# The last two rows of an output projection, taken bank by bank, and a running total of squares over seven banks

## What is computed

```python
def rms_norm(x, g):
    xf = x.astype(jnp.float32)
    y = xf * lax.rsqrt(jnp.mean(xf * xf, axis=-1, keepdims=True) + EPS)
    return (y * g.astype(jnp.float32)).astype(x.dtype)

for l in range(DEPTH):                                  # DEPTH = 2
    ...
    mixed = jnp.concatenate([y, m_out], axis=-1) @ w_out[l]
    h = h + rms_norm(mixed, norm_mix_post[l])
    f = swiglu_ffn(rms_norm(h, norm_ffn_pre[l]), w_ffn_in[l], w_ffn_out[l])
    h = h + rms_norm(f, norm_ffn_post[l])
...
# second block
y, yc = token_mix(h, hc, lp, with_ctx)                  # ends in ... @ w_out
x = x + gate1 * rmsnorm(y, g_post_mix[l])
```

## Time and profile before

| | us |
|---|---|
| median of 3 runs | 1951.76 |
| lowest and highest run | 1950.09, 1953.26 |
| span of the profiled execution | 1947.3 |
| PE busy (matmuls) | 1814.3 (93% of the span) |
| DVE busy | 1216.2 (62%) |
| ACT busy | 896.1 (46%) |
| POOL busy | 125.7 (6%) |

### The profile page before, as it was taken

The page is one execution under the profiler, slowest core; times in us unless marked ns, Lnnn a source line. Parts: engine busy times, 40 slices in busy tenths (PEclk is TensorE's granted clock), DMA queues, the critical chain, the costliest instruction groups (busy, mean ns, idle before and its releaser), DMA issues.

```text
span 1947.3 us, 25641 instructions
## 1 busy us (share of the span) xinstructions
PE 1814.3 (93%) x9201; PEld 1507.9 (77%) x9201; DVE 1216.2 (62%) x2170; ACT 896.1 (46%) x1452; POOL 125.7 (6%) x137
## 2 busy tenths in 40 slices
PE   7997999999999997899999999799987989999997
PEld 7875788888887865678888888678576878888885
DVE  3554668887323656456865532564575479889888
ACT  3446443222213445543223221342383368888885
POOL 1000000000000000000110000120000210110102
PEclk8898999999999998999999999799998879999999
DMA  4223225455333124024655423330011359999995
GB/s 150 87 76 115 87 64 142 134 145 147 107 96 96 44 65 184 23 65 137 182 159 149 119 93 97 112 89 22 21 67 66 108 222 377 395 385 370 386 372 187
DMA packets 203854, 289.32 MB, mean 149 GB/s; under 512 B 12332, under 2 KB 150548, under 8 KB 203636
## 3 DMA queue, kind: packets, MB, share of 16 engines
q1 hardware_dynamic: 188788, 239.56, 36.9%
q0 software_dynamic: 11920, 36.48, 6.1%
q10 hardware_dynamic: 3056, 12.06, 1.6%
HBM read 271.77 MB, written 21.53 MB: 151 GB/s over the span
## 4 chain that ended last, share of the span: by engine, by line
PE 85%; DVE 7%; ACT 6%; issue 1%; DMA 1%; POOL 0%; DVEq 0%; ACTq 0%; POOLq 0%
PE bank L200 23%; PE bank L202 23%; PE bank L201 23%; PE bank L69 11%; PE bank L654 2%; DVE weights_low L227 1%; PE bank L2195 1%; ACT weights_high L221 1%; DVE tmp L69 1%; DVE z_and_u L69 1%; DVE ring L69 1%; PE bank L1651 1%; ACT spare L69 1%; PE bank L2544 1%; PE bank L272 1%
## 5 line engine op out<-in xcount | busy, mean ns | idle before, releaser
L227 DVE TENSOR_TENSOR weights_low<-ring,weights_high 128x1024 fp32r<-128x1024 f32 x202 | 246.7, 1223 | 395.3 <-ACT weights_high L221 394.8
L200 PE MATMUL bank<-XH,weights_high 128*128 128x512 f32 x1056 | 423.2, 401 | 17.8 <-DVE weights_low L227 6.5
L202 PE MATMUL bank<-XH,weights_low 128*128 128x512 f32 x1056 | 415.6, 394 | 0.0
L201 PE MATMUL bank<-XL,weights_high 128*128 128x512 f32 x1056 | 415.2, 393 | 0.0
L221 ACT CAST weights_high<-ring 128x1024 fp32r<-128x1024 f32 x202 | 211.1, 1047 | 432.6 <-PE bank L202 422.8
L200 PEld LDWEIGHTS bank<-XH,weights_high 128*128 128x128 f32 x1056 | 200.8, 190 | 63.0 <-DVE weights_low L227 9.6
L202 PEld LDWEIGHTS bank<-XH,weights_low 128*128 128x128 f32 x1056 | 200.7, 190 | 43.4
L201 PEld LDWEIGHTS bank<-XL,weights_high 128*128 128x128 f32 x1056 | 201.1, 190 | 40.3 <-issue 0.5
L2235 DVE TENSOR_TENSOR XL<-ring,XH 128x1024 fp32r<-128x1024 f32 x144 | 169.8, 1219 | 11.7 <-ACT XH L2229 11.7
L2229 ACT CAST XH<-ring 128x1024 fp32r<-128x1024 f32 x144 | 145.2, 1048 | 0.6 <-PE bank L202 0.6
L69 DVE SCALAR_TENSOR_TENSOR squares<-ring,c_silu,squares 128x128 f32<-128x128 f32 x384 | 135.2, 352 | 13.6
(11 more groups left out here) (506 smaller groups left out, 3263.2 us busy)
## 6 DMA issues: line engine op xcount, KB each, us to landing
ring<-in_w_ffn_in SPq DMA_DIRECT2D x88, 512.0 KB, 4.7
ring<-in_w_gate SPq DMA_DIRECT2D x72, 512.0 KB, 5.4
ring<-in_w_up SPq DMA_DIRECT2D x72, 512.0 KB, 7.3
ring<-in_w_down SPq DMA_DIRECT2D x72, 512.0 KB, 5.9
ring<-in_w_ada POOLq DMA_DIRECT2D x48, 512.0 KB, 4.7
ring<-in_w_ffn_out SPq DMA_DIRECT2D x44, 512.0 KB, 3.6
ring<-in_w_out SPq DMA_DIRECT2D x24, 512.0 KB, 3.6
slot_output<-expert_out SPq DMA_DIRECT2D x18, 512.0 KB, 6.7
```

Of the source, the lines that this page charges most:

```text
L200: PE.matmul(out_ap, w_h, x_h, start=first, stop=False, skip_group_check=True)
L201: PE.matmul(out_ap, w_h, x_l, start=False, stop=False, skip_group_check=True)
L202: return PE.matmul(out_ap, w_l, x_h, start=False, stop=last, skip_group_check=True)
L227: V.tensor_tensor(wl[:, s, :], ring[s][:, :], wh[:, s, :].bitcast(F32), ALU.subtract).then_inc(split_done.sem, 1)
```

## The change

The last unit of an output projection, rows s=0 and s=1, is no longer done row by row. A new function `rows_closing` does both rows after both weight halves are ready to be used: banks 0 to 3 of row 0, banks 0 to 3 of row 1, and then bank 4 of row 0 and of row 1, bank 5 of both, 6 of both, 7 of both. chunk_done goes up with row 1's product of banks 0 to 6, used_done with bank 7 of row 0 and with bank 7 of row 1. The running total takes in bank 6 too, and PE multiplies two parts with ones, the total first. All five projections use it; `rows_root` is otherwise as it was.

```diff
@@ stream
+                    if closing and i == units - 1:
+                        if s == 1:
+                            closing()
+                    elif paired and i == 0:
-                    if paired and i == 0:
...
@@ rows_products
-                closing = i == units - 1 and s == 1
-                for c in range(KC) if closing else (2, 3, 6, 0, 1, 7, 4, 5):
+                for c in (2, 3, 6, 0, 1, 7, 4, 5):
...
+        def rows_closing(unit, xh, xl, ready=None, order=None, tokens=None):
+            def closing():
+                for s, c in (*((0, c) for c in range(4)), *((1, c) for c in range(4)),
+                             *((s, c) for c in range(4, KC) for s in range(2))):
+                    row = order[2 * unit + s] if order else 2 * unit + s
+                    if c == 0:
+                        if ready:
+                            PE.wait_ge(ready.sem, row + 1)
+                        if tokens:
+                            pe.need(tokens[row])
+                        PE.wait_ge(split_done.sem, used_done.n + s + 1)
+                    last = three_pass(bank[c][:, :], wh[:, s, c * P:(c + 1) * P], wl[:, s, c * P:(c + 1) * P],
+                                      xh[:, row, :], xl[:, row, :], False, False)
+                    if c == KC - 1:
+                        last.then_inc(used_done.sem, 1)
+                    elif s == 1:
                         last.then_inc(chunk_done.sem, 1)
                         chunk_done.n += 1
+                used_done.n += 2
+            return closing
...
@@ rows_root
-                elif 1 < c < KC - 2:
+                elif 1 < c < KC - 1:
...
-            parts = ((squares[(KC - 2) % 4], squared[KC - 2]), (squares[(KC - 1) % 4], squared[KC - 1]),
-                     (total, added[KC - 3]))
+            parts = ((total, added[KC - 2]), (squares[(KC - 1) % 4], squared[KC - 1]))
```

More of the change, by code:

```diff
@@ L288, in opener, with stream @@
             return lambda s: open_half(src, s)
-        def stream(units, src, products, evacuate=None, side=None, then=None, fused=None, beside=None, paired=None):
+        def stream(units, src, products, evacuate=None, side=None, then=None, fused=None, beside=None, paired=None, closing=None):
             pending = []
@@ L410, in token_products, with rows_products @@
             used_done.n += 2
-        def rows_products(units, xh, xl, ready=None, order=None, tokens=None, between=None):
+        def rows_products(xh, xl, ready=None, order=None, tokens=None, between=None):
             def products(i, s, first):
@@ L429, in products @@
                                       xl[:, row, :], first and s == 0, False)
-                    if closing and c < KC - 1:
+                return last
+            return products
+        def rows_closing(unit, xh, xl, ready=None, order=None, tokens=None):
[14 more added lines that the diff above has]
+                    elif s == 1:
                         last.then_inc(chunk_done.sem, 1)
                         chunk_done.n += 1
-                return last
-            return products
+                used_done.n += 2
+            return closing
         def evac_to(tile, n, scale=None, order=None, done=None):
@@ L576, in rows_root @@
                     tok = pe.do(PE.matmul, bank[0][:, t:t + 1], part[:, t * P:(t + 1) * P], ones[:, 0:1],
-                                start=n + t == 0, stop=n == 2, skip_group_check=True)
+                                start=n + t == 0, stop=n == 1, skip_group_check=True)
             if floor is None:
@@ L1215, in ffn @@
             root_table()
-            stream(FC // 2, rows, rows_products(FC // 2, HH, HL, low_part), beside)
+            stream(FC // 2, rows, rows_products(HH, HL, low_part), beside,
+                   closing=rows_closing(FC // 2 - 1, HH, HL, low_part))
             spread = rows_root(root_floor[:, :], next_src)
@@ L1226, in mix_out @@
                 root_table()
-            stream(KC // 2, rows_src(w, order), rows_products(KC // 2, XH, XL, order=order, tokens=tokens, between=between),
-                   beside=beside)
+            stream(KC // 2, rows_src(w, order), rows_products(XH, XL, order=order, tokens=tokens, between=between),
+                   beside=beside, closing=rows_closing(KC // 2 - 1, XH, XL, order=order, tokens=tokens))
             return rows_root(None, next_src)
```

## The result

The changed kernel takes 1980.66 us (median of 4 runs, 1978.30 to 1982.40) against 1950.92 (4 runs, 1948.62 to 1953.26): 1.015 times the time before, 95% interval 1.0135 to 1.0164. That is 29.7 us more, and 1981.6 was forecast. The span of the profiled execution is 1979.9 us against 1947.3.

The account below looks back on a forecast made before the run. TensorE was taken as the bound, 85% of the span's chain. Terms 28.4 + 1.8 - 0.9 + 0.5 gave +29.8 us on a median of 1951.76, so 1981.6; range 1972.5 to 1987.

Parts of the forecast that it names:

- The held cast: At four places ScalarE's cast of the next weights waits for row 0's increment until E-0.63, all eight squares behind it.
- The sequence behind it: After the cast: squares, additions, then ones-matmuls ending at E+10.04 instead of E+2.87; +7.17 us at three places, +6.88 at the first.
- The clock: At the four held places TensorE idles over 6 us, so ones-matmuls run at 1.2 GHz; slower spread at two places, +1.8 us.
- the -0.9 of the fifth place: Fifth place, without a cast: two groups of ones-matmuls end at E+1.98 instead of E+2.87, saving 0.9 us.
- The earlier need of the last half: Row s=1 of the last unit starts earlier and waits for its weights_low: 0.1 us at each of five places, +0.5.
- The sum: All terms at the five places together: +29.8 us, giving 1981.6 us for the median of the runs.
- 28.4 + 1.8 - 0.9: Later ones-matmuls at four places 28.4 us, slower spread at two places 1.8, group saved at the fifth place -0.9.
- The clock did not hold: Rival at the held places: ones-matmuls still run at 2.4 GHz and no spread slows, +21.4 us, 1973.1; chance 7%.
- The low clock behind: Rival in the four following stages: low clock lasts longer, and the earlier need costs 0.3; 1986 to 1988 us, chance 5%.
- the gain: Rival at the closings: squares are not held, by an early increment or passing the cast; -4.2 us, 1947.6, chance 4%.
- The longer total: Seven banks in the total: one more VectorE addition, one ones-group less, saving 0.89 us if ready by E+0.06.

Follow-up runs that it names:

- e1: Kernel before the change, with only the used_done increment of row 0 moved to the first matmul of bank 7 of row 1: 1979.68 us.
- e4: Changed kernel with ScalarE's cast of the next first half put between the squares of banks 6 and 7: 1944.08 us, ratio 0.9957 to the kernel before.
- e6: Changed kernel with 24 unused matmuls added after bank 7 at each of the four held places: 1970.27 us, ratio 1.0093 to the kernel before.
- e5: Changed kernel with ScalarE's cast of the next first half put between the squares of banks 3 and 4: 1968.88 us, ratio 1.0079 to the kernel before.
- e7: Kernel before the change, with the new closing at the fifth place only, which has no cast: 1950.81 us, ratio 1.000.
- e10: Same kernel as e4, run again on another occasion: 1944.31 us against 1950.98, ratio 0.9969.
- e8: Kernel before the change, with only the cast of the next first half moved between the squares of banks 6 and 7: 1954.45 us, ratio 1.001.
- e3: Kernel before the change, with the seven-bank total and two groups of ones-matmuls, row order and increment kept: 1959.56 us, ratio 1.0039.

## Why the prediction was right

**The held cast.** Right in place and time. The cast starts at 632.87, and E (last matmul's start plus 0.43) is 633.50: E-0.63, as worked out. e1 shows that this wait alone is enough, e4 that without it nothing of the loss is left.

**The sequence behind it.** The first square came at E+0.32, not 0.42, because it starts before the cast's end is recorded; the first addition at E+1.53 for 1.65, the ones-matmuls at E+6.35 for 6.46, their end at E+9.90 for 10.04 (second place). From the last matmul to the spread this makes +7.02 us at the second, third and fourth place against +7.17 forecast. At the first it is +7.11 against +6.88: there the second addition comes 1.14 us after the first and not 0.79 (DVE 238.87, then 240.01), as it also did before (1.15). I had carried the second place's spacing over to it.

**The clock.** Ones-matmuls and spread ran at half clock at all four places, as taken: the clock fell 3.0 to 4.9 us after the last matmul there, with PE idle. e6 gives back 7.6 us of it in the stretches. Not foreseen was its part at the fifth place. Slices there, columns as above:

```profile
1567.00:1568.00 1.00, 1.00 (x11) 1.00 0.00 0
1568.00:1569.00 1.00, 0.74 (x7) 0.90 0.00 0
1569.00:1570.00 1.00, 0.60 (x3) 0.50 0.00 0
```

The clock fell at about 1568.8, 2.5 us after the start of the last wide matmul, while ones-matmuls ran, and the spread took 2.04 us instead of 1.13. So the -0.9 of the fifth place was given back at once: its stretch is 8.14 against 8.07. In e4, e5, e6, e7 and e10 the clock held there until after the spread and some 0.84 us were kept. That term was right as a wait and missed a clock that can fall early; in the sum it is +0.9 us. It is no effect of the change alone, since in e8 the clock fell as early at this place with the order of before.

**The earlier need of the last half.** 0.4 us in all, for 0.5: the 48 matmuls of the last unit take 0.08 to 0.11 us more than before at four places, from first start to last, and 0.02 at the third. Banks follow each other every 0.68 us, and at the second place of the changed kernel the one after the new wait came after 0.75 (624.80 to 625.55), three more after some 0.69.

**The sum.** To the spread's end the prediction had 28.4 + 1.8 - 0.9 = 29.3 us for the five places; they gave 30.0 to the first matmul behind: 30.0 at the four held ones, forecast 30.2, and 0.07 at the fifth, forecast -0.9. That the median grew by 29.7 us where 29.8 was forecast is in part luck: the interval of the ratio allows 26 to 32 us, and the two profiles differ by 32.6. The mechanism, its place and the size of each wait are not luck.

**The rivals.** The clock did not hold. The low clock behind did not grow the stages that follow the four held places: they changed by -1.1, -2.5, -0.3 and +1.8 us, which is no loss in sum. The squares did not pass the waiting cast, so the gain did not come. One figure in that last rival is off: the cast would have to start 5.4 us earlier than E-0.63 to break even, and the text calls this where it started before; before, it started at 618.53, which is E-5.39, only 4.8 us earlier. The forecast does not use it.

**The longer total.** The prediction lets it save a group only if it is ready by E+0.06. With the new order and the cast out of the way it is (e4: the first group starts 0.54 us after the last matmul). e3 shows what comes of it where it is not met. The expectation of e3 had the total ready at E+0.84, because it left out the wait for the addition before; it was ready at E+1.86.

## What to carry to other kernels

When matmuls are reordered, look for every semaphore that is raised along them, and for what is queued behind the waits on each: a buffer that is given back 4.8 us later costs nothing in its own right, and 7 us if an engine waits for it ahead of work on the path. The same order of matmuls with the same total was worth +30 us or -7 us here, by where one cast of 1 us stood in another engine's queue. And a chain of additions that runs at 0.8 us a piece behind banks of 0.68 had no room for one more here until its input came earlier.

## What the runs showed of the hardware that was not expected

- Where ones-matmuls (128x1) followed the last wide matmul at once, the granted clock fell from 2.4 GHz to 1.2 at 2.4 to 5.5 us after its start, at different places of one kernel and at one place in different kernels (fifth place: 2.50 in the changed kernel, 2.52 in e8, 5.25 before, 5.29 in e5). With PE kept at wide matmuls for 5.4 us more (e6), it fell 8.7 to 10.8 us after bank 7's last. That scatter moves a spread between 1.13 and 2.05 us.
- An ACT instruction that waits for nothing but the cast ahead of it on ACT starts about 0.1 us before that cast's recorded end (cast 632.87 to 633.92, square at 633.82).
